# Two-layer hybrid transformer block on one core: squares, Gram products and value transposes of the recurrence gathered in fewer, longer runs

## What is computed

```python
qkv = _causal_conv_silu(b_qkv, conv_w)            # q, k, v of the recurrence: 3 x 1024 features
bq, bk = _l2norm(bq), _l2norm(bk)                 # by head, 8 heads of 128
m = where(strict, einsum('bhnid,bhnjd->bhnij', k_beta, k) * decay, 0)
attn = einsum('bhnid,bhnjd->bhnij', q, k) * decay
sol = triangular_solve(m + eye, concatenate([v_beta, k_beta * exp(g_cum)], -1))
...
y = sigmoid(g_a) * y_a + sigmoid(g_b) * y_b
return y @ w_out
```

## Time and profile before

| | |
|---|---|
| median of 3 runs | 1101.5 us (1101.43 to 1101.6) |
| span of the profiled execution | 1099.9 us, 19903 instructions |
| time of the runs less the profiled span | 1.6 us, what lies around the first and last instruction |
| PE busy | 1089.6 us (99%), 8135 instructions |
| DVE / ACT / POOL busy | 559.5 / 561.2 / 670.2 us |
| DMA | 183.37 MB, mean 167 GB/s |
| mean granted TensorE clock | 0.999 of full speed |

### The profile page before, as it was taken

The page is one execution under the profiler, slowest core; times in us unless marked ns, Lnnn a source line. Parts: engine busy times, 40 slices in busy tenths (PEclk is TensorE's granted clock), DMA queues, the critical chain, the costliest instruction groups (busy, mean ns, idle before and its releaser), DMA issues.

```text
span 1099.9 us, 19903 instructions
## 1 busy us (share of the span) xinstructions
PE 1089.6 (99%) x8135; PEld 1014.0 (92%) x8138; DVE 559.5 (51%) x1082; ACT 561.2 (51%) x888; POOL 670.2 (61%) x351
## 2 busy tenths in 40 slices
PE   8999999999999999999999999999999999999997
PEld 7999999998898999999999999999989979999996
DVE  6788479354515631223358866793644344212234
ACT  7645864435655544444464567544356554444442
POOL 4876769627673457654377758685378454586442
PEclk9999999999999999999999999999999999999999
DMA  7443544624543655555555444445155255555553
GB/s 291 173 154 135 188 130 163 180 74 170 194 153 125 205 188 186 180 189 180 184 173 173 157 141 164 152 156 163 69 194 194 97 181 178 191 179 187 187 180 112
DMA packets 63337, 183.37 MB, mean 167 GB/s; under 512 B 18576, under 2 KB 19088, under 8 KB 63248
## 3 DMA queue, kind: packets, MB, share of 16 engines
q1 hardware_dynamic: 47936, 172.48, 45.3%
q10 hardware_dynamic: 15312, 9.64, 3.4%
HBM read 179.47 MB, written 2.62 MB: 166 GB/s over the span
## 4 chain that ended last, share of the span: by engine, by line
PE 97%; ACT 1%; DVE 1%; DMA 1%; POOL 0%; issue 0%; SPq 0%; DVEq 0%; ACTq 0%; POOLq 0%
PE psum L494 28%; PE psum L495 27%; PE psum L496 27%; PE psum L658 1%; PE psum L985 1%; PE psum L964 1%; PE psum L699 1%; PE psum L1086 1%; PE psum L588 1%; PE psum L879 1%; PE psum L872 1%; PE psum L754 1%; DMA sb_raw<-weights 1%; PE psum L682 1%; PE psum L843 0%; PE psum L670 0%
## 5 line engine op out<-in xcount | busy, mean ns | idle before, releaser
L391 POOL TENSOR_TENSOR sb_low<-sb_raw,sb_high 128x1024 fp32r<-128x1024 f32 x257 | 616.5, 2413 | 337.3 <-ACT sb_high L381 323.1
L381 ACT ACTIVATE sb_high<-sb_raw 128x1024 fp32r<-128x1024 f32 x322 | 340.1, 1061 | 406.4 <-DMA sb_raw<-weights 361.6
L494 PE MATMUL psum<-sb_h_high,sb_high 128*128 128x256 f32 x1640 | 463.9, 283 | 0.0
L495 PE MATMUL psum<-sb_h_low,sb_high 128*128 128x256 f32 x1640 | 463.3, 282 | 0.0
L496 PE MATMUL psum<-sb_h_high,sb_low 128*128 128x256 f32 x1640 | 462.5, 282 | 0.0
L494 PEld LDWEIGHTS psum<-sb_h_high,sb_high 128*128 128x128 f32 x1640 | 310.3, 189 | 1.8 <-DVE sb_region_c L1879 0.3
L496 PEld LDWEIGHTS psum<-sb_h_high,sb_low 128*128 128x128 f32 x1640 | 308.6, 188 | 0.0
L495 PEld LDWEIGHTS psum<-sb_h_low,sb_high 128*128 128x128 f32 x1640 | 307.7, 188 | 0.9
L391 DVE TENSOR_TENSOR sb_low<-sb_raw,sb_high 128x1024 fp32r<-128x1024 f32 x65 | 85.4, 1314 | 95.4 <-ACT sb_high L381 95.0
L1992 DVE SCALAR_TENSOR_TENSOR sb_conv<-psum,sb_param,sb_conv 128x255 f32<-128x255 f32 (+1 forms) x144 | 58.2, 473 | 37.0 <-ACT sb_conv L1405 36.8
L2248 DVE SCALAR_TENSOR_TENSOR sb_sq<-sb_th,psum 128x512 f32<-128x512 f32 x22 | 15.1, 687 | 110.0 <-ACT sb_th L1610 110.0
(11 more groups left out here) (307 smaller groups left out, 1549.0 us busy)
## 6 DMA issues: line engine op xcount, KB each, us to landing
sb_raw<-weights SPq DMA_DIRECT2D x322, 512.0 KB, 3.2
sb_pre_gain<-pre_gains ACTq DMA_DIRECT2D x6, 512.0 KB, 4.4
sb_post_gain<-post_gains ACTq DMA_DIRECT2D x6, 512.0 KB, 4.5
sb_kx<-mem SPq DMA_DIRECT2D x2, 512.0 KB, 4.4
sb_x<-x SPq DMA_DIRECT2D x1, 1024.0 KB, 10.7
t_dram<-sb_sq ACTq DMA_DIRECT2D x4, 256.0 KB, 2.9
out<-sb_x SPq DMA_DIRECT2D x4, 256.0 KB, 2.0
m_dram<-sb_m ACTq DMA_DIRECT2D x8, 64.0 KB, 2.1
```

The lines of the kernel that those rows point to most:

```text
L381: nc.scalar.activation(high[:, n % HIGHS, :], raw[:, n % RAWS, :], ACT.Copy).then_inc(high_ready, 1)
L391: eng.tensor_tensor(low[:, k, :], raw[:, k, :], high[:, n % HIGHS, :].bitcast(F32), ALU.subtract).then_inc(low_ready[k], 1)
L494: pe.matmul(out, a[0], b[0], start=start, stop=False, **kw)
L495: pe.matmul(out, a[0], b[1], start=False, stop=False, **kw)
```

## The change

Only the order of TensorE's stream changes; no instruction is added or removed. The squares of slots 4 and 5 go together behind the slab bv 0, with all four kk products; those of 6 and 7 go behind bv 2. The kq products go in pairs ahead of ga 0 and ga 2. The value transposes go behind gb 0 (one), gb 2 (two) and gb 3 (one). The streams of DVE, ACT, POOL and SP hold the same instructions in the same order as before.

```diff
                 for i in range(4):
                     wide(("bv", i), h, (dve_conv, ("tap", 0, 8 + i)), ((2, 3, 4, 0)[i],))
-                    squares(4 + i)
+                    if i % 2 == 0:
+                        squares(4 + i)
+                        squares(5 + i)
                     if i == 2:
                         softmax_transposes()
-                    if i < 2:
+                    if i == 0:
                         pe.wait_ge(*dve_conv.at(layer, ("silu", 3)))
-                        for g in (2 * i, 2 * i + 1):
+                        for g in range(4):
                             gram("kk", g, 0, ((0, 1, 5, 6)[g],))
...
                 for g in range(4):
-                    gram("kq", g, 8, beside)
+                    if g % 2 == 0:
+                        gram("kq", g, 8, beside)
+                        gram("kq", g + 1, 8, beside)
                     wide(("ga", g), h, (act_gate, ("ga", g)), beside)
...
+                def values_by_token(g):
+                    c, hh = g // 2, g % 2
+                    what = ("v_tok", g)
+                    o = claim(what, (dve_gdn, what), beside)
+                    for i in range(4):
+                        tr = pe.transpose(o[:, i * P:(i + 1) * P], conv[:, 16 + 4 * hh + i, c * P:(c + 1) * P], ident)
+                    tr.then_inc(pe_gdn.sem, mark(pe_gdn, what))
+
                 for g in range(4):
                     wide(("gb", g), h, (act_gate, ("gb", g)), beside)
                     if g == 0:
                         attended()
-                    c, hh = g // 2, g % 2
-                    what = ("v_tok", g)
-                    o = claim(what, (dve_gdn, what), beside)
-                    if g == 0:
                         pe.wait_ge(*dve_conv.at(layer, ("silu", 11)))
-                    for i in range(4):
-                        tr = pe.transpose(o[:, i * P:(i + 1) * P], conv[:, 16 + 4 * hh + i, c * P:(c + 1) * P], ident)
-                    tr.then_inc(pe_gdn.sem, mark(pe_gdn, what))
+                        values_by_token(0)
+                    if g == 2:
+                        values_by_token(1)
+                        values_by_token(2)
+                    if g == 3:
+                        values_by_token(3)
```

## The result

The changed kernel took 1116.55 us (median of 4 runs, 1116.23 to 1119.9) where the one before took 1101.51; the ratio is 1.0141, with a 95% interval of 1.0129 to 1.0153. Forecast were 1114.1 us and 1108.8 to 1117.8. The profiled execution has a span of 1114.4 us and 1116.27 us as a run, so 1.9 us lie around the span.

The account below looks back on a forecast made before the run. PE, busy for 99% of the span, was taken to bound the kernel. Switches 0, stalls +10.9 and clock +1.7 made 12.6 us on 1101.5, so 1114.1 us, range 1108.8 to 1117.8.

Parts of the forecast that it names:

- What bounds the kernel: Whole kernel: PE is busy 99% of the span, so whatever lengthens or shortens its own stream shows in full.
- The removed switches, taken at 0: Eight fp32 runs gone from between PE's slabs: saving taken as 0, at most 0.64 us.
- The wait for bank 0 at ga 0: PE waits at ga 0 in each layer until DVE's taps 11 free bank 0: 4.1 us in layer 0 if DVE didn't move.
- The late DVE: Later bv 1 delays DVE's taps 11 by 1.4 and 1.55 us, making the stalls 5.5 and 5.4, together 10.9 us.
- The clock: Behind the ga 0 stalls PE's clock may fall to half: one fall of two taken, 1.7 us, bounds 0 and 4.8.
- the single row at the end of the span: Trace end, only row on idle gaps: clock fell to half 4.7 us behind PE's last matmul.
- The bound of 2.4 us for one fall: From the trace's start: 4.8 us at half speed from the first matmul, costing half of that, 2.4 us.
- The stall without the late DVE: At ga 0, bv 1's delay is swallowed: stalls of 4.1 and 3.8 us, 1109.4 us in all; chance 0.13.
- The small stall behind ACT's last tap 11: At ga 0, rk doesn't hold DVE, taps 11 follow ACT: stalls of 3.45 us each, 1108.4 us; chance 0.05.
- dear switches: Between PE's slabs: not slower, since gathering pays; needs 1.4 us per removed switch to outweigh the stall; chance 0.04.
- No other new wait of PE over 0.3 us: Sign in the list of PE's waits: besides the two at ga 0, some 5 us each, none new over 0.3 us.

Follow-up runs that it names:

- run 7: Kernel before with each kq product's four fp32 matmuls spread over its ga slab, 24 more switches in all, banks as before: 1101.55 us, ratio 0.9997.
- run 10: Full changed order with the banks chosen by hand and rk ahead of one low piece on POOL: 1102.19 us, ratio 1.0001.
- run 4: Kernel before, order kept, only two results' banks exchanged (ga 0 takes bank 0, kq 1 bank 4): 1115.72 us, ratio 1.0125.
- run 1: Full changed order with only the PSUM banks of the kq products and ga slabs chosen by hand: 1103.0 us, ratio 1.0013.
- run 6: Full change with rk ahead of one low piece on POOL instead of behind it: 1111.29 us, ratio 1.0084.
- run 3: Kernel before with only the kq products in pairs: 1112.61 us, ratio 1.0101.
- run 9: Kernel before with only the squares and kk products moved as in the change: 1103.9 us, ratio 1.0015.
- run 2: Full change with its kq part undone, one kq product ahead of each ga slab again: 1104.41 us, ratio 1.0031.

## Why the prediction was right, point by point

- **What bounds the kernel.** Right: each stall and each slow matmul of PE came out in the time in full (14.55 us in the rows, 14.5 in the span).
- **The removed switches, taken at 0.** Right, and now shown from both sides: 24 more switches 0.9997 (run 7), eight fewer 1.0001 (run 10). What the slab's first matmul loses, the last fp32 row gives back.
- **The wait for bank 0 at ga 0.** Right in place, releaser and count. Run 4 shows that the bank alone does it, run 1 that without it the stall is gone.
- **The late DVE.** Right in its links; run 6 confirms the one through POOL, and runs 3 and 9 that the squares and kk products are its cause. The term was a little too large: DVE was 1.45 us late at taps 9 (148.98 - 147.14 - 0.39), for 1.4, but only 1.27 at taps 11, since the four DMA issues took 2.00 us instead of 2.19; and the way from DVE's end to PE's start was 0.06 us, not 0.2. Stalls of 5.16 and 5.20 us were forecast as 5.5 and 5.4, together 10.4 instead of 10.9.
- **The clock.** The mechanism was right and the size too small; this is the term that the forecast missed by: 4.2 us where 1.7 was taken. The step that failed is the one that went by the single row at the end of the span, where the clock fell 4.7 us behind the last matmul, so that two falls behind stalls of 5.4 us looked like a toss-up. In the changed kernel the clock fell about 3.1 and 2.6 us behind PE's last matmul, and in all eight unfilled stalls of the profiles (5.2, 5.2, 4.2, 3.7, 4.6, 4.6, 3.4 and 3.4 us) it fell, at a cost of 1.3 to 2.7 us each. The bound of 2.4 us for one fall, from the start of the span, was passed once. What the Trainium skill says of an idle gap (TensorE: Matmul & The Clock Gate, "HAM oscillation — how this bites in real kernels"), that the clock goes back to half behind it, held in every one of these rows. With 10.4 for the stalls and 4.2 for the clock the sum would have been 1116.1 on the median of before. The forecast is nearer than this term deserves: the stalls were taken 0.5 us too long and the clock 2.5 us too short.
- **The rivals.** The stall without the late DVE is what run 3 made, with the stalls that it named but with the clock's falls, which that rival had left out. The small stall behind ACT's last tap 11 is run 6: 3.42 us against 3.45. The rival on the other side, dear switches, is refuted by run 7.
- **Not foreseen:** hidden under the large stall lay a second weak place. Where the stall is mended and DVE still late, PE waits at gb 1 or at the attention products; those kernels lose 1.3 to 2.7 us in all (runs 1, 2 and 9). In runs 2 and 9 the starts at kq 1 and gb 1 account for 2.1 us; in run 1 only part of the loss was located. "No other new wait of PE over 0.3 us" came true in the changed kernel, where PE came 5 us late.

## What to carry to other kernels

Ahead of moving work between two steps of a rotating pool of buffers, write down which buffer each result gets before and after: here the order looked harmless and the wait came from one slab taking the bank of the slab just ahead, and exchanging two banks without moving anything cost nearly as much (14.0 us for 15.0). Read the price of a switch from starts on both sides of it before paying for fewer switches. And when an engine with a gated clock is made to wait for a few us, add the slow stretch behind the wait to the wait.

## What the runs showed of the hardware that was not expected

The cost of a fall of TensorE's clock does not follow the length of the stall: 3.42 us of stall lost 2.66 us behind it in one layer and 1.52 in the other of the same execution, 4.16 us lost 1.29, 5.16 lost 2.23. It follows how long the half clock lasts once PE is at work again: read from windows as above, 5.06 and 4.46 us of such work in the two layers of the changed kernel lost 2.23 and 1.96, 6.03 us in layer 0 of run 6 lost 2.66, and the 2.9 to 3.4 us of the other five lost 1.3 to 1.5. That is a little under half of it each time.

Nor does the fall come at a fixed distance: it came 2.4 to 5.3 us behind the last matmul ahead of the stall, where the prediction went by the one distance of 4.7. In run 4 the clock fell, in both layers, only after PE was at work again: ga 0 started at 167.35, and the window from 166 to 168 still has the full clock, the next one 0.52.

```profile
164.00:166.00 2.00, 0.00 (x0) 1.00 0.00 0
166.00:168.00 2.00, 0.65 (x5) 1.00 0.00 0
168.00:170.00 2.00, 2.00 (x12) 0.52 0.52 131
170.00:172.00 2.00, 2.00 (x13) 0.63 0.00 0
```

Executions with a stall also differ from each other: the four of run 3 lie 3.5 us apart (1111.42 to 1114.88). By itself that says little, since the kernel before spread by 1.7 us in that comparison (17 executions) but by 3.4 in the last one (35, 1101.3 to 1104.7). But in runs 3, 4 and 6 the order of the times is that of the mean granted clock on record, the longer execution never at the higher clock (from the shortest on): 0.997, 0.997, 0.996 and 0.992 in run 3; 0.996, 0.996, 0.994 and 0.993 in run 4; 0.998, 0.996, 0.996 and 0.994 in run 6. How much of the spread the falls make was not measured.
